# Normalised activations turned and rounded in token halves, narrow projections in column tiles, and a new order at the start of the delta stage

## The reference: two layers of mixer and feed-forward

```python
    for layer in range(DEPTH):
        ...
            mix = _even_mixer(x, ev_w_in[i], ev_gla_w_a2[i], ev_gla_b_a[i], ev_gla_norm_g[i],
                              ev_swa_sinks[i], ev_w_out[i])
        ...
        x = _layer_norm(ALPHA * x + mix, ln1_g[layer], ln1_b[layer])
        x = _layer_norm(ALPHA * x + _swiglu(x, ffn_w_gate[layer], ffn_w_up[layer], ffn_w_down[layer]),
                        ln2_g[layer], ln2_b[layer])
```

```python
    gam = jnp.exp(jnp.where(causal, decay[..., :, None] - decay[..., None, :], -jnp.inf))
```

## Time and profile before

| | |
|---|---|
| median of 3 runs | 1301.32 us (1300.08 to 1302.7) |
| the profiled execution | 1301.35 us |
| its span, first to last instruction | 1299.5 us |
| mean granted TensorE clock | 0.995 |
| PE / DVE / ACT / POOL busy | 98% / 36% / 33% / 47% |
| matmul instructions | 7102 |

### The profile page before, as it was taken

The page is one execution under the profiler, slowest core; times in us unless marked ns, Lnnn a source line. Parts: engine busy times, 40 slices in busy tenths (PEclk is TensorE's granted clock), DMA queues, the critical chain, the costliest instruction groups (busy, mean ns, idle before and its releaser), DMA issues.

```text
span 1299.5 us, 16971 instructions
## 1 busy us (share of the span) xinstructions
PE 1269.7 (98%) x7102; PEld 1043.9 (80%) x7102; DVE 468.4 (36%) x769; ACT 430.3 (33%) x579; POOL 611.0 (47%) x297
## 2 busy tenths in 40 slices
PE   9999999999999999998999899999999999999997
PEld 8878877888888888876877778887788888888885
DVE  5548855211111100125688945563530101010105
ACT  4264533322222221224544335442422222222111
POOL 4342143964444343537744347463595444435341
PEclk9999999999999999999999989999999999999999
DMA  9221022333233332232233342012133333323221
GB/s 319 90 66 65 1 94 102 98 97 99 96 98 97 101 132 92 98 98 69 89 99 97 97 82 74 9 66 86 47 126 99 97 97 98 97 81 131 81 97 65
DMA packets 108463, 121.13 MB, mean 93 GB/s; under 512 B 20018, under 2 KB 83876, under 8 KB 108388
## 3 DMA queue, kind: packets, MB, share of 16 engines
q1 hardware_dynamic: 101156, 116.84, 28.4%
q10 hardware_dynamic: 7232, 3.21, 1.0%
HBM read 116.15 MB, written 3.67 MB: 92 GB/s over the span
## 4 chain that ended last, share of the span: by engine, by line
PE 88%; DVE 5%; issue 3%; POOL 2%; ACT 1%; DVEq 0%; POOLq 0%; ACTq 0%
PE bank L1556 27%; PE bank L1557 26%; PE bank L1558 26%; PE bank L1880 3%; POOL w_lo L621 1%; DVE KH L1340 1%; DVE f_ab L1069 1%; DVE OO L1318 1%; DVE SS L1316 1%; PE bank L1752 1%; PE bank L1703 0%; PE bank L1826 0%; PE bank L1763 0%; PE bank L1994 0%; PE bank L1744 0%
## 5 line engine op out<-in xcount | busy, mean ns | idle before, releaser
L621 POOL TENSOR_TENSOR w_lo<-w_raw,w_hi 128x1024 fp32r<-128x1024 f32 (+1 forms) x202 | 471.5, 2357 | 496.0 <-ACT w_hi L766 496.0
L1556 PE MATMUL bank<-x_hi,w_hi 128*128 128x512 f32 x936 | 367.3, 392 | 7.3 <-DVE f_ab L1069 3.8
L1557 PE MATMUL bank<-x_lo,w_hi 128*128 128x512 f32 x936 | 364.9, 390 | 0.0
L1558 PE MATMUL bank<-x_hi,w_lo 128*128 128x512 f32 x936 | 364.9, 390 | 0.0
L766 ACT ACTIVATE w_hi<-w_raw 128x1024 fp32r<-128x1024 f32 (+1 forms) x202 | 197.4, 1027 | 219.4 <-issue 170.5
L1556 PEld LDWEIGHTS bank<-x_hi,w_hi 128*128 128x128 f32 x936 | 176.0, 188 | 46.7 <-issue 7.6
L1558 PEld LDWEIGHTS bank<-x_hi,w_lo 128*128 128x128 f32 x936 | 176.0, 188 | 36.7
L1557 PEld LDWEIGHTS bank<-x_lo,w_hi 128*128 128x128 f32 x936 | 176.0, 188 | 35.8
L1136 DVE TENSOR_TENSOR f_ab<-bank,f_ab 128x512 f32<-128x512 f32 x44 | 30.4, 692 | 369.0 <-PE bank L1558 369.0
L1556 PE MATMUL bank<-w_hi,h_hi 128*128 128x512 f32 x352 | 139.4, 396 | 1.5 <-POOL w_lo L621 1.5
L1558 PE MATMUL bank<-w_hi,h_lo 128*128 128x512 f32 x352 | 139.2, 396 | 0.0
(11 more groups left out here) (272 smaller groups left out, 1218.9 us busy)
## 6 DMA issues: line engine op xcount, KB each, us to landing
w_raw<-ffn_w_gate_dram SPq DMA_DIRECT2D x22, 1024.0 KB, 5.3
w_raw<-ffn_w_up_dram SPq DMA_DIRECT2D x22, 1024.0 KB, 5.3
w_raw<-ffn_w_down_dram SPq DMA_DIRECT2D x20, 1024.0 KB, 5.0
w_raw<-od_w_in_dram SPq DMA_DIRECT2D x16, 1024.0 KB, 5.7
w_raw<-ev_w_in_dram SPq DMA_DIRECT2D x8, 1024.0 KB, 5.5
w_raw<-ev_w_out_dram SPq DMA_DIRECT2D x4, 1024.0 KB, 5.1
w_raw<-od_w_out_dram SPq DMA_DIRECT2D x4, 1024.0 KB, 5.4
x_fm<-x_fm_dram SPq DMA_DIRECT2D x8, 256.0 KB, 6.7
```

The lines of the kernel that those rows point to most:

```text
L621: pool.tensor_tensor(w_lo[:, b % 2, c], w_raw[:, b % 2, c], w_hi[:, b % 2, c].bitcast(F32), ALU.subtract).then_inc(w_lo_ready, 1)
L1556: pe.matmul(out_ap, st[0], mv_[0], start=start, stop=False)
L1557: pe.matmul(out_ap, st[0], mv_[1], start=False, stop=False)
L1558: return pe.matmul(out_ap, st[1], mv_[0], start=False, stop=stop)
```

## The change

**LN 1 to 3 in token halves.** `turn_x(i, half)` turns two tiles; bank `("xT", i, half, j)` holds channel groups 2j and 2j+1 of 256 tokens, 4 banks a half. Half 0 is turned inside the GEMM before, ahead of the last tile's products from its channel group 1 on (`early`); half 1 is turned between the two halves of the first gate or conv block, which is now 96 matmuls of 256 columns instead of 48 of 512. DVE makes two instructions of 256 columns for each j (L1100 of the changed kernel) and for even j waits for ACT's `x_hi` and subtracts `x_lo` at once (L1106); POOL does that for odd j (L668), and between the halves it does the next weight block's `w_lo`. DVE's `round_x(i, 0)` stands behind tile 2's normalisation and ahead of tile 3's add. The ring of banks is set back at `ba_fm` instead of at the first convolution.

**Narrow products.** `few_columns` computes `ga` and `ba` in fp32 from 32 weight columns: 16 matmuls of 512 columns (a fp32 matmul runs as two instructions) that go to four groups of 32 output partitions in turn; the four partial sums are added by the product that reads them (`g_a2` four times, `o_eye32`). The blocks, roundings and subtractions of both are gone. `gstate` writes its odd heads to partitions 64 to 127.

**The decay rows.** `drow`, its subtraction on DVE and `prepare` on POOL are gone. One extra product gives the decay as rows, they go to DRAM, and for each t SP reads them back to all partitions of `GU` (512 KB). ACT takes `EE` from `GU`, and `GT` in 8 instructions of one head with a bias.

**Orders.** At t = 0: half a filler, grams, kTM, the other half, then the waits, vTM. The last GEMM's last two blocks go tile 0, tile 1, tile 0, tile 1, then tiles 2 and 3.

```diff
-            u += filler(-1) + both("kTM", "vTM", "drow") + filler(0) + gram + both("qk") + filler(1) + m1 + filler(2) + ds
+            u += filler(-1) + gram + both("kTM", "vTM") + filler(0) + both("qk") + filler(1) + m1 + filler(2) + ds
         else:
-            u += gram + both("kTM", "vTM") + m1 + both("drow") + ds + both("qk") + filler(1) + both("kS")
+            u += gram + both("kTM", "vTM") + m1 + ds + both("qk") + filler(1) + both("kS")
...
-        if key == ("conv", CONV_ORDER[0]):
+        if key == ("ba_fm",):
...
-            layer_norm(1)
+            layer_norm(1, range(3))
+            round_x(1, 0)
+            layer_norm(1, (3,))
             split_to(first_block[("gate", 0, 0)] + 1)
-            round_x(1)
+            round_x(1, 1)
 
...
+            def load_rows(t):
+
+                if t == 0:
+                    sp.wait_ge(s["dec_rows_ready"], 1)
+                    sp.dma_start(dec_dram, dec_rows[:, :]).then_inc(s["dec_rows_out"], 16)
+                    sp.wait_ge(s["dec_rows_out"], 16)
+                    full(sp, ("dr32", 1))
+                else:
+                    sp.wait_ge(s["e_ready"], 2 * t)
+                    sp.wait_ge(s["gt_arg"], 2 * t)
+                sp.dma_start(GU[:, :, :].rearrange("p h c -> p (h c)"),
+                             dec_dram[t * GDN_H:(t + 1) * GDN_H, :].rearrange("h c -> (h c)").unsqueeze(0).broadcast_to([P, GDN_H * P]))\
+                  .then_inc(s["rows_landed"], 16)
...
-                    full(act, ("drow", t, hg))
-                    act.activation(EE[:, hsl[hg], :], fm4(("drow", t, hg)), ACT.Exp).then_inc(s["e_ready"], 1)
+                    act.activation(EE[:, hsl[hg], :], GU[:, hsl[hg], :], ACT.Exp).then_inc(s["e_ready"], 1)
                 for hg in range(2):
                     act.wait_ge(s["gt_arg"], 2 * t + hg + 1)
-                    act.activation(GT[:, hsl[hg], :], GT[:, hsl[hg], :], ACT.Exp).then_inc(s["gt_exp"], 1)
+                    for h in range(4 * hg, 4 * hg + 4):
+                        ins = act.activation(GT[:, h, :], GT[:, h, :], ACT.Exp, bias=ndec[:, t, h:h + 1])
+                    ins.then_inc(s["gt_exp"], 1)
...
-                def low(k):
-                    dve.wait_ge(s["x_hi_ready"], KD * i + k + 1)
-                    dve.tensor_tensor(x_lo[:, k, :], f_ab[:, k % 4, :], x_hi[:, k, :].bitcast(F32), ALU.subtract)\
-                       .then_inc(s[("x_lo_even", "x_lo_odd")[k % 2]], 1)
-
-                for k in range(KD):
-                    full(dve, ("xT", i, k))
-                    if k >= 4:
-                        low_part_there(dve, i, k - 4)
-                    src = bank(("xT", i, k))[:, :]
-                    take(dve.tensor_scalar(f_ab[:, k % 4, :], src, lnc[:, gcol + k:gcol + k + 1],
-                                           lnc[:, gcol + 16 + k:gcol + 17 + k], ALU.mult, ALU.add), ("xT", i, k))
-                    if k % 2:
-                        low(k - 1)
+                cols = token_halves[half]
+                for j in range(KD // 2):
+                    key = ("xT", i, half, j)
+                    full(dve, key)
+                    if half:
+                        half_part_there(dve, i, 0, 2 * j)
+                    for k in (2 * j, 2 * j + 1):
+                        part = slice(k % 2 * 256, (k % 2 + 1) * 256)
+                        ins = dve.tensor_scalar(f_ab[:, j, part], bank(key)[:, part], lnc[:, gcol + k:gcol + k + 1],
+                                                lnc[:, gcol + 16 + k:gcol + 17 + k], ALU.mult, ALU.add)
+                    take(ins, key)
+                    if j % 2 == 0:
+                        taken(dve, key)
+                        high_parts_there(dve, i, half, j)
+                        dve.tensor_tensor(x_lo[:, 2 * j:2 * j + 2, cols], f_ab[:, j, :].rearrange("p (k n) -> p k n", k=2),
+                                          x_hi[:, 2 * j:2 * j + 2, cols].bitcast(F32), ALU.subtract)\
+                           .then_inc(s["x_lo_even"], 1)
 
...
-                            if i == 4:
-                                normalise(t)
-                            elif t:
-                                normalise(t - 1)
-                if i < 4:
-                    normalise(NT - 1)
+                            if i < 4 and t == 0:
+                                continue
+                            if i < 4 and t == 1:
+                                normalise(0)
+                            normalise(t)
+                            if i < 4 and t >= 2:
+                                round_x(i, t - 2)
...
+                for half in range(2) if fresh is not None else ():
+                    if half:
+                        turn_x(fresh, 1)
+                    cols = token_halves[half]
+                    for k in range(KD):
+                        if half == 0:
+                            weights_there(b, k)
+                        half_part_there(pe, fresh, half, k)
+                        for n in range(len(keys)):
+                            ps = fill(keys[n]) if half == 0 and k == 0 else bank(keys[n])
+                            ins = mm3(ps[:, cols], weights(b, k, n * P, P), xcols(k, cols), k == 0, k == KD - 1)
+                            if half and k == KD - 1:
+                                done(ins, keys[n])
                 if fresh is not None:
...
+            def few_columns(key, w):
+
+                ps = fill(key)
+                quarters = P // SB
+                for j, x in enumerate((x_hi, x_lo)):
+                    for k in range(KD):
+                        q = k % quarters
+                        ins = pe.matmul(ps[q * SB:(q + 1) * SB, :], w[:, k, :], x[:, k, :].bitcast(F32),
+                                        start=j == 0 and k < quarters, stop=j == 1 and k >= KD - quarters,
+                                        skip_group_check=True)
+                done(ins, key)
+
...
+                        if early is not None and k0 + nk == kt and (kk, t) == (1, tiles[-1]):
+                            early()
...
+                for t, bb in [(0, b), (1, b), (0, b + 1), (1, b + 1)] + [(t, bb) for t in range(2, NT) for bb in (b, b + 1)]:
...
-            def turn_x(i):
-
-                for t in range(NT):
+            def turn_x(i, half):
+
+                for t in (2 * half, 2 * half + 1):
                     pe.wait_ge(s["z_norm"], NT * (i - 1) + t + 1)
                     for k in range(KD):
-                        ps = fill(("xT", i, k)) if t == 0 else bank(("xT", i, k))
-                        ins = pe.transpose(ps[:, tile_cols[t]], x_tm[:, t, k * P:(k + 1) * P], eye[:, :])
-                        if t == NT - 1:
-                            done(ins, ("xT", i, k))
+                        key = ("xT", i, half, k // 2)
+                        ps = fill(key) if t % 2 == 0 and k % 2 == 0 else bank(key)
+                        col = k % 2 * 256 + t % 2 * P
+                        ins = pe.transpose(ps[:, col:col + P], x_tm[:, t, k * P:(k + 1) * P], eye[:, :])
+                        if t % 2 and k % 2:
+                            done(ins, key)
 
...
-                filler(t, -1)
-                if t == 0:
-                    pe.wait_ge(s["conv_silu"], len(CONV_ORDER))
+                filler(t, -1, 0, 4)
...
-                if t:
-                    grams()
+                grams()
                 for hg in H:
                     per_head(("kTM", t, hg), lambda o, h: pe.transpose(o, qkv[:, KD + h, tc_], eye[:, :]))
+                filler(t, -1, 4, 8)
+                if t == 0:
+                    pe.wait_ge(s["conv_silu"], len(CONV_ORDER))
+                    pe.wait_ge(s["t_blk_ready"], 1)
                 for hg in H:
                     per_head(("vTM", t, hg), lambda o, h: pe.transpose(o, qkv[:, 2 * KD + h, tc_], eye[:, :]))
-                if t == 0:
-                    pe.wait_ge(s["t_blk_ready"], 1)
-                else:
+                if t:
                     small_product()
-                for hg in H:
-                    pe.wait_ge(s["gu_ready"], 2 * t + hg + 1)
-                    ps = fill(("drow", t, hg))
-                    done(mul(ps[:, :], ones[:, :].broadcast_to([P, P]),
-                             GU[:, hsl[hg], :].rearrange("p a b -> p (a b)")), ("drow", t, hg))
```

210 lines of the change are left out of this document (105 added, 105 removed).

## The result

| | before | after |
|---|---|---|
| median | 1300.88 us (4 runs) | 1308.83 us (4 runs, 1307.4 to 1310.57) |
| ratio after/before | | 1.006 [1.0042, 1.0077] |
| profiled execution, its span | 1301.35, 1299.5 | 1308.78, 1307.0 |
| mean granted clock of TensorE | 0.995 | 0.988 |

The account below looks back on a forecast made before the run. PE, busy 98% of the span, was taken to bound the kernel. Gains of −15.6 us against losses of +22.2 (+19.2 at the LNs, +3 clock) gave net +6.6 on 1301.35: 1308 us, range 1295 to 1318.

Parts of the forecast that it names:

- The halves lose the overlap in which DVE scaled the next group while ACT rounded this one: LN 1: DVE waits for ACT in each even pair; both halves take 14.4 us, against 9.8 for all before.
- 19.2: Loss summed over the LN boundaries: +7.7 us at LN 1, +3.8 at LN 2, +7.7 at LN 3; bounds 12 and 30.
- a half at 7.2: LN 1: DVE's time for the pairs of one half, 2.5 us per even pair and 1.1 per odd pair.
- 30.5: LN 1: time from DVE's add of tile 1 to the gate block's end at 237.1 us, +7.7 against before.
- The meeting of DVE and POOL: LN 1: half 1's first `x_lo` runs beside POOL's `w_lo` and is there at 228.9 instead of 228.3.
- LN 2, 3.8: LN 2: tile 1's add at 576.02 plus LN 1's 30.5 gives a block end at 606.5, +3.8 us.
- +3 for the clock: All LNs: new PE gaps of 3 us let the clock fall, costing 3 us in all; bounds 0 and 9.
- Rival D: `ga` and `ba`: narrow products do not run side by side, +8.9 us each, 1330; two side by side 1315; chance 0.08.
- −3.8, −2.6, −4.2 forecast: Gains in us: `drow` gone at t = 1 to 3; `gstate` pairs side by side; start of the delta stage.
- the second of the two cases given: Delta stage's start: filler(0,1) starts at 762.9 if the clock falls, against 760.8 if it stays.
- the −0.4 at the gate blocks: Behind the first gate blocks: two waits of PE for `w_lo` go, about 0.2 us each.
- Rival C: LNs: PE's earlier start (3 us each) counts and half 1 is ready when needed: 1277, half of that 1290; chance 0.15.

Follow-up runs that it names:

- Experiment 8: The kernel of experiment 1, with DVE subtracting an even group's low part at once instead of after the next group's scaling: 1298.79 us, ratio 0.9982.
- experiment 2: The changed kernel, halves kept, with DVE scaling the odd pair before it subtracts the even pair's low part: 1295.62 us, ratio 0.9964.
- experiment 1: The changed kernel with LN 1 to 3 as before (no halves, old turning, rounding, bank plan and first blocks): 1287.43 us, ratio 0.9898.
- Experiment 3: The changed kernel, with POOL doing half 1's low parts before the next block's `w_lo`: 1309.59 us, ratio 1.0071.
- experiment 4: The changed kernel, with 16 products without use ahead of half 0 and 20 ahead of half 1 at each LN: 1307.17 us, ratio 1.0048.
- experiment 6: The kernel of experiment 2, with ACT rounding the next block's weights ahead of tile 3's layer norm: 1295.11 us, ratio 0.996.
- 11: The kernel of experiment 10 with 17 instead of 28 filling products ahead of tile 3's turn: 1291.24 us, ratio 0.9929.
- experiment 9: The kernel of experiment 2, with all four tiles added, normalised and turned before both halves are scaled and rounded in succession: 1295.96 us, ratio 0.9964.
- experiment 10: The kernel of experiment 9 with both gaps filled, by 28 products of 128 columns and 13 of 256: 1291.55 us, ratio 0.9928.

## Why the prediction was right, step by step

**The mechanism.** "The halves lose the overlap in which DVE scaled the next group while ACT rounded this one" was the step on which it stood. Experiment 8 shows it without any halves (+11.4), experiment 2 with them (−13.2, of which some is the clock), experiment 1 shows that everything else gains. At LN 1, where the clock cost nothing, the 7.9 us are 4.4 for this step (30.9 to 26.5) and 3.5 for the rest of the halves, which the forecast had as the second wait of PE and as narrower scalings. The net forecast of the three boundaries with their clock, 19.2 − 0.4 + 3 = 21.8, stands against 22.0 in the table and 21.4 in experiment 1. That it is so close is partly luck, as the terms below show.

**The steps of LN 1.** A pair was priced at 1.05 and takes 0.99; a half at 7.2 and takes 7.35; the wait of half 1 from 225.8 to 228.9 was to be 3.1 and is 2.78; from tile 1's add to the end 30.5, measured 30.9. The meeting of DVE and POOL was priced at 0.6 and costs 0.9 (1.58 against 0.69) at LN 1, 0.17 at LN 2. Experiment 3 takes it away and the median does not fall; at LN 1 it came back as a wait for `w_lo`.

**Mis-sized: LN 2, 3.8 against 5.6.** The forecast carried LN 1's 30.5 over; the chain there is 32.3 (579.35 to 611.67). The clock fell in its half 0 too, PE was still busy with that when tile 3 was ready, and DVE waited 2.61 for half 1's turn instead of 1.86 (LN 1). 1.0 of the 1.8 is the clock, by experiment 4, and so is 0.75 of LN 3's 1.1 too much. The forecast had these in a term of their own, **+3 for the clock**, which was too large: 1.75 by experiment 4. The chain itself was too small: with the gaps filled it is 30.9, 31.3 and 30.9 against 30.5, together 1.6. The two errors cancel, by luck.

**Narrow products.** Rival D is out: `few_columns` starts 0.11 apart, 32 instructions in 3.58 us (611.67 to 615.25); forecast 3.7, so −1.9 came out as −2.0 at `ba`. In a row at the 0.45 of the earlier trace rows they would be 14.4, four times as long. The Trainium skill, "TensorE: Matmul & The Clock Gate", part 3, has 3.07 times for four row tiles and no figure for four column tiles; by 3.07 the 14.4 would be an estimated 4.7. The trace, with 3.58 for four column tiles, is faster than that, and the measurement decides.

**`drow`, `gstate`, t = 0.** −3.8, −2.6, −4.2 forecast, −3.9, −3.0, −4.3 measured; at t = 1 PE waits 0.52 for DVE ahead of `ds`, forecast about 0.6. At t = 0 the clock fell (0.71 from 757 to 762). That was the second of the two cases given, and it was priced at 762.9 − 766.22 = −3.3; the −4.2 stood between the cases, and the measured −4.3 is 1.0 better than its own case.

**Not foreseen.** At the first product behind the attention PE, by then 5.6 us earlier, was earlier than POOL: a wait of 1.13 for `w_lo`, so 1.1 of what the start and `gstate` had won is given back at once. Behind `ba`, the products that spread it and an extra decay product cost 1.0. Against both, the start and the attention came out 0.8 better; why stays open. The rest of the change was forecast at −15.2 (all gains but the −0.4 at the gate blocks) and gained 13.4 by experiment 1, 14.5 by the table.

**Rival C,** that PE's earlier start would count, needed tile 3's z by 217. It came at 219.2 in a kernel that ran 4.5 us ahead of the one before, thus where 223.7 was against the forecast's 223; PE's start of half 0 at 211.37 was indeed early, and it bought nothing, because half 1 stood behind it.

## What to carry to other kernels

When two engines hand a tile back and forth, the order inside one engine's program is worth more than the size of the pieces: let it start the next piece before it waits for the answer to this one. Here that order cost 11 to 13 us at three places (the clock's part in it included), while the smaller pieces, which were to start the next stage sooner, started only the part of it that was not the bound. Before a stage is cut in halves, write down who must be done before the second half can begin; an engine that is fed at the first half and starved at the second ends when the second does. And a removed wait should be followed one engine further: three times here (experiments 3, 6 and 11) it came back as another one.

## What the runs showed of the hardware

- **DVE and GpSimd beside each other.** A `tensor_scalar` from SBUF to SBUF of 1024 columns took 2.04 us instead of 0.81 beside POOL's subtraction (experiment 6, at all three LNs); the forecast had reckoned only with DVE operations of two SBUF inputs. The Trainium skill, "SBUF — State Buffer", section "Who interferes with whom", names `tensor_scalar` among the operations that can take the port pair shared with GpSimd, when its operands allow it; the run agrees. The same operation from a bank of PSUM (`f_ab<-bank`) kept its 0.99 a pair while POOL was at work.
- **Short gaps and the clock.** In the changed kernel a gap of 2.07 and one of 1.45, 3 us later, left LN 1's half 0 at full clock. In experiment 9 gaps of 1.91 and 1.74 with only 8 transposes between them brought 0.58 over the next 6 us. In experiment 2 gaps of 2.30 and 3.30 left the clock at 1.00 at LN 1, while 2.15 and 3.38 around the same work at LN 2 brought 0.69 (598 to 602); in experiment 6 the gap of 2.29 at LN 1, behind the same work as experiment 2's 2.30, brought 0.79 (211 to 219). So neither the length of a gap nor the work around it was enough here to tell whether the clock falls. Where the gaps were filled (experiments 4, 10 and 11) it stayed at 1.00 in every first block.
- **Four column groups of 32 run fully side by side** at 512 fp32 columns: `few_columns` starts 0.112 us apart, a quarter of the 0.45 of the earlier trace rows.
- **Narrow fp32r products.** One of 128 columns took 0.12 us (28 in 3.33, experiment 10), like one of 256 (0.12 between two starts), while 512 take 0.23.
